# Neighbourhood attention: the scores are made two turns ahead, and queued on TensorE right in front of a turn's values

## The reference, cut to what matters

```python
z = h @ w_in[l]                                    # (1024, 1024) @ (1024, 2560)
a, gate, q, k, v = jnp.split(z, splits, axis=-1)
conv_out = conformer_conv(a, gate, ...)            # 31 taps over the positions, 512 channels
q = rms_norm(q.reshape(B, S, N_HEADS, HEAD_DIM), q_norm_g[l])
k = rms_norm(k.reshape(B, S, N_HEADS, HEAD_DIM), k_norm_g[l])
...
# each query sees an 8 x 16 window of keys, clamped inside the grid
s = jnp.einsum("bqhd,brqchd->bhqrc", q_r, k_win) * scale
s = s + bias                                       # learned, by 2-D offset
p = jax.nn.softmax(s, axis=(-2, -1))
out = jnp.einsum("bhqrc,brqchd->bqhd", p, v_win)
...
mix = jnp.concatenate([conv_out, attn_out], axis=-1)
x = x + mix @ w_out[l]
```

## Time and profile before

| what | value |
|---|---|
| median of 3 runs | 2429.26 us |
| the profiled execution | 2429.0 us, its span 2427.2 us |
| VectorE's first `scores_in` to its ninth (turn 0 to turn 8) | 146.15 to 216.43 us |
| pair 1, likewise | 216.43 to 287.52 us |
| pair 2, likewise | 287.52 to 359.77 us |
| from there to the first matmul that waits for the mixed input's low part | 359.77 to 442.26 us |

### The profile page before, as it was taken

One profiled execution on the slowest core, in us unless ns is written; L12 is line 12 of the kernel. 1 busy time (PEld: TensorE's weight loads), 2 busy tenths in 40 slices (PEclk: granted clock), 3 DMA queues, 4 the chain that ended last, 5 costly groups with the idle time before them and its releaser, 6 DMA issues. The chain is left out here.

```text
span 2427.2 us, 28938 instructions
## 1 busy us (share of the span) xinstructions
PE 2298.8 (95%) x10276; PEld 1765.5 (73%) x10276; DVE 1605.5 (66%) x1904; ACT 1096.1 (45%) x1779; POOL 1170.5 (48%) x834
## 2 busy tenths in 40 slices
PE   8988886899999999999999999997999999999999
PEld 6865553777888888788775665583788888888887
DVE  7888884288666666646766666747866665544587
ACT  5145554345545443322326666615666662222342
POOL 1000000257887787878521111232777777777732
PEclk9989997999999999999999999998999999999999
DMA  3211100421443436894310000032466668976412
GB/s 130 69 34 26 29 23 9 148 78 46 180 174 113 182 130 245 318 381 157 126 35 18 27 18 14 27 139 87 173 253 258 253 257 324 360 279 266 149 33 85
DMA packets 89166, 342.90 MB, mean 141 GB/s; under 512 B 22401, under 2 KB 23169, under 8 KB 76097
## 3 DMA queue, kind: packets, MB, share of 16 engines
q1 hardware_dynamic: 88368, 336.65, 36.8%
q10 hardware_dynamic: 656, 4.41, 0.5%
HBM read 224.16 MB, written 116.27 MB: 140 GB/s over the span
## 5 line engine op out<-in xcount | busy, mean ns | idle before, releaser
L1101 PE MATMUL ps<-operand,turn_weights 128*128 128x512 f32 x3192 | 736.3, 392 | 16.3 <-POOL turn_weights L728 5.5
L1101 PEld LDWEIGHTS ps<-operand,turn_weights 128*128 128x128 f32 x3192 | 600.6, 189 | 150.7 <-issue 14.4
L728 POOL TENSOR_TENSOR turn_weights<-turn_raw,turn_weights 128x512 fp32r<-128x512 f32 (+1 forms) x330 | 445.0, 1359 | 225.5 <-ACT turn_weights L1563 224.9
L1101 PE MATMUL ps<-hidden_operand,turn_weights 128*128 128x512 f32 x2268 | 517.5, 390 | 3.3 <-issue 1.4
L1101 PEld LDWEIGHTS ps<-hidden_operand,turn_weights 128*128 128x128 f32 x2268 | 424.8, 188 | 95.8 <-issue 6.0
L2756 DVE TENSOR_TENSOR branch_out<-ps,branch_out 128x1024 f32<-128x1024 f32 x172 | 210.5, 1224 | 201.3 <-PE ps L1101 200.3
L690 POOL TENSOR_TENSOR weight_hi<-weight_raw,zero_col 128x1024 fp32r<-128x1024 f32 (+1 forms) x27 | 54.6, 2023 | 582.1 <-PE ps L1007 409.8
L1563 ACT ACTIVATE turn_weights<-turn_raw 128x512 fp32r<-128x512 f32 (+1 forms) x330 | 204.9, 623 | 267.1 <-PE ps L1101 252.3
L842 PE MATMUL ps<-input_hi,weight_hi 128*128 128x512 f32 x592 | 196.2, 413 | 21.3 <-DVE input_lo L2335 10.4
L842 PE MATMUL ps<-input_lo,weight_hi 128*128 128x512 f32 x656 | 205.9, 395 | 0.0
L842 PE MATMUL ps<-input_hi,weight_lo 128*128 128x512 f32 x592 | 185.3, 395 | 0.0
(11 more groups left out here) (351 smaller groups left out, 3579.9 us busy)
## 6 DMA issues: line engine op xcount, KB each, us to landing
hidden_operand<-hidden_kept SPq DMA_DIRECT2D x91, 1024.0 KB, 7.8
hidden_kept<-hidden_parts SPq DMA_DIRECT2D x54, 1024.0 KB, 8.7
hidden_kept<-hidden_parts SPq DMA_DIRECT2D x27, 1536.0 KB, 6.2
turn_raw<-w_ff SPq DMA_DIRECT2D x40, 512.0 KB, 4.1
turn_raw<-w_mlp SPq DMA_DIRECT2D x32, 512.0 KB, 4.3
turn_raw<-w_mlpd SPq DMA_DIRECT2D x32, 512.0 KB, 4.4
turn_raw<-w_ffd SPq DMA_DIRECT2D x20, 512.0 KB, 4.6
weight_raw<-w_out SPq DMA_DIRECT2D x16, 512.0 KB, 3.6
```

Of the source, the lines that this page charges most:

```text
L728: pool_.tensor_tensor(place(p, 1), place(p, 1, WT) if raw is None else raw, bits(place(p, 0)), ALU.subtract).then_inc(s["st_lo"], 1)
L1101: ins = mm(PS[:, b, :], weights(p, w, k), tokens(p, a, k), start=(FRESH[p] and k == 0 and step == 0), stop=(k == n - 1 and step == 2), ski ...
```

## The change

`scores(n+2)`, no longer `scores(n+1)`, is made in turn n, and it stands behind the slots 0, 1 and 2, right in front of `values(n)`. Turn 6 makes none (the next pair's q and k aren't there), and turn 7 makes two: `scores(n+1)` behind `turn(n, 0)`, and `scores(n+2)` in front of `values(n)`. VectorE's `probs(n+1)` and `first_part` now stand ahead of `scores_in(n+2)`, and `second_part` behind it. ScalarE makes `exps(n+2)` at the end of a turn, and the `weight_hi` of a turn behind `head_guess`. The pieces, the taps and the transposes of v are dealt out anew, in the same number. In pair 3 `ln_sums` for the mean stands in turn 1 and not in turn 0.

```diff
-BESIDE = (((0, 1), (2,), (), (3,)),
+BESIDE = (((0,), (1,), (2,), (3,)),
           ((4,), (5,), (6,), (7,)),
           ((), (8, 9), (10,), ("m0", 11)),
-          ((12,), (13,), (14,), (15, "m1")),
-          ((), (16, 17), (), ("m2",)),
-          ((18,), (19,), (), ("m3",)),
-          ((20,), (21,), (), (22,)),
-          ((), (23,), (), ()))
+          ((12,), (13, "m1"), (14,), (15,)),
+          ((), (), (16,), ("m2", 17)),
+          ((18,), (19, "m3"), (20,), ()),
+          ((21,), (22,), (23,), ()),
+          ((), (), (), ()))
...
-            for what in BESIDE[0][0] + BESIDE[0][1] + BESIDE[0][3]:
+            for what in (0, 1):
                 next_piece(0, what)
             scores(0)
+            for what in (2, 3):
+                next_piece(0, what)
+            scores(1)
+            v_turn(0, 0)
...
+                    ahead = n + 2 < 4 * CBLOCKS
                     turn(n, 0)
-                    if j < CBLOCKS - 1:
+                    if ahead and j == 7:
                         scores(n + 1)
-                    if j == 1:
-                        v_turn(c, 1)
                     slot(0)
                     turn(n, 1)
+                    if j == 0:
+                        v_turn(c, 1)
                     slot(1)
                     if c == 3 and j >= 3:
                         output_part(j)
-                    if j == CBLOCKS - 1 and c < 3:
-                        scores(n + 1)
-                    if j == 0:
-                        v_turn(c, 0)
                     slot(2)
-                    values(n)
-                    slot(3)
-                    if c == 3 and j == 0:
+                    if ahead and j != 6:
+                        scores(n + 2)
+                    if c == 3 and j == 1:
                         ...
                         ln_sums(lambda m: Y[:, m, :], "ln_mean")
+                    values(n)
+                    slot(3)
+                    if j == CBLOCKS - 1 and c < 3:
+                        v_turn(c + 1, 0)
```

ScalarE, the order of a turn:

```diff
                     probs_t(n, 0)
-                    if more:
-                        exps(n + 1, 0)
-                        exps(n + 1, 1)
...
+                    if more and not new_pair:
+                        probs_scale(n + 1, 0)
                     probs_t(n, 1)
+                    if more and not new_pair:
+                        probs_scale(n + 1, 1)
...
                         if j == 2:
                             head_square(c + 1, 0)
-                            weight_hi(U_QKV + 3 * c + 5)
                         elif j == 4:
                             head_square(c + 1, 1)
-                            weight_hi(U_QKV + 3 * c + 6)
...
+                    if ahead and j < 6:
+                        exps(n + 2, 0)
+                        exps(n + 2, 1)
+                    elif new_pair:
+                        exps(n + 1, 0)
+                        exps(n + 1, 1)
                         probs_scale(n + 1, 0)
                         probs_scale(n + 1, 1)
+                        exps(n + 2, 0)
+                        exps(n + 2, 1)
                     if c < 3:
                         if j in (2, 3, 4, 5):
                             head_guess(4 * c + 2 + j, 5)
                         elif j == 6:
                             head_hi(c + 1, 1)
+                        if j == 2:
+                            weight_hi(U_QKV + 3 * c + 5)
+                        elif j == 4:
+                            weight_hi(U_QKV + 3 * c + 6)
                         elif j == 7:
                             weight_hi(U_QKV + 3 * c + 7)
```

More of the change, by code:

```diff
@@ L1062, in _ @@
                         ln_sums(lambda m: Y[:, m, :], "ln_mean")
-                    elif c == 3 and j == 3:
+                    values(n)
+                    slot(3)
+                    if j == CBLOCKS - 1 and c < 3:
+                        v_turn(c + 1, 0)
+                    if c == 3 and j == 3:
                         pe.wait_ge(s["ln_sq"], 4)
@@ L1702, in _ @@
             probs_scale(0, 1)
+            exps(1, 0)
+            exps(1, 1)
             for c in range(4):
@@ L1705, in _ @@
                     n = CBLOCKS * c + j
-                    more = n < 4 * CBLOCKS - 1
+                    more, ahead = n + 1 < 4 * CBLOCKS, n + 2 < 4 * CBLOCKS
+                    new_pair = more and j == 7
                     probs_t(n, 0)
-                    if more:
-                        exps(n + 1, 0)
-                        exps(n + 1, 1)
[L1711 to L1714, removed]
+                    if j == 0:
+                        v_copy(c, 0)
+                        if c:
+                            attn_out(c - 1, 0)
+                            attn_out(c - 1, 1)
+                    if more and not new_pair:
+                        probs_scale(n + 1, 0)
+                    probs_t(n, 1)
+                    if more and not new_pair:
+                        probs_scale(n + 1, 1)
+                    if j == 0:
                         v_copy(c, 1)
@@ L1739, in _ @@
                             head_hi(c + 1, 1)
+                        if j == 2:
+                            weight_hi(U_QKV + 3 * c + 5)
+                        elif j == 4:
+                            weight_hi(U_QKV + 3 * c + 6)
                         elif j == 7:
                             weight_hi(U_QKV + 3 * c + 7)
-                    elif j == 3:
+                    elif j == 2:
+                        for m in range(4):
+                            act.wait_ge(s["ln_cent"], m + 1)
+                            act_.activation(LT[m][:], Y[:, m, :], ACT.Square).then_inc(s["ln_sq"], 1)
+                    elif j == 4:
                         for h in range(2):
@@ L2369, in conv @@
             def conv(n):
-                for _ in range(n):
+                for _ in range(min(n, 4 * TAPS - tap[0])):
                     c, t = divmod(tap[0], TAPS)
@@ L2473, in _ @@
             probs(0, 1)
+            scores_in(1, 0)
+            scores_in(1, 1)
             conv(2)
             def first_part(c, j):
-                if j == 0 and c:
-                    weight_lo(U_QKV + 3 * c + 4)
+                if j == 0:
+                    if c:
+                        weight_lo(U_QKV + 3 * c + 4)
+                    conv(1)
                 elif j == 1:
-                    conv(1)
+                    conv(2)
                 elif j == 2:
                     evac(c + 1, 0, 0)
+                    conv(1)
                 elif j == 3:
@@ L2487, in first_part @@
                     evac(c + 1, 1, 0)
+                    head_norm(4 * c + 5, 5)
                 elif j == 5:
-                    weight_lo(U_QKV + 3 * c + 6)
                     head_norm(4 * c + 6, 5)
@@ L2492, in first_part @@
                     head_norm(4 * c + 7, 5)
-                elif j == 7:
-                    head_lo(c + 1, 1)
+                    conv(1)
             def second_part(c, j):
@@ L2498, in second_part @@
                     weight_lo(U_QKV + 3 * c + 5)
-                elif j == 4:
-                    head_norm(4 * c + 5, 5)
+                elif j == 5:
+                    weight_lo(U_QKV + 3 * c + 6)
                 elif j == 6:
                     head_lo(c + 1, 0)
-                elif j == 7:
-                    evac(c + 1, 2, 0)
-                conv(min((4, 4, 3, 3, 2, 3, 3, 4)[j], 4 * TAPS - tap[0]))
+                    conv(1)
+                    head_lo(c + 1, 1)
+                conv((3, 3, 2, 4, 3, 3, 0, 1)[j])
             def last_pair(j):
                 if j == 0:
+                    conv(4 * TAPS - tap[0])
                     weight_lo(U_OUT + 1)
-                    conv(4 * TAPS - tap[0])
                 elif j == 1:
@@ L2532, in _ @@
                     n = CBLOCKS * c + j
-                    more = n < 4 * CBLOCKS - 1
-                    if more and j < CBLOCKS - 1:
+                    if j == CBLOCKS - 1 and c < 3:
+                        conv(2)
                         scores_in(n + 1, 0)
                         scores_in(n + 1, 1)
+                        evac(c + 1, 2, 0)
+                        conv(1)
+                        probs(n + 1, 0)
+                        probs(n + 1, 1)
+                        scores_in(n + 2, 0)
+                        scores_in(n + 2, 1)
+                        second_part(c, j)
+                        continue
+                    if n + 1 < 4 * CBLOCKS:
+                        probs(n + 1, 0)
+                        probs(n + 1, 1)
                     if c < 3:
                         first_part(c, j)
[L2539 to L2546, removed]
+                    if j < 6:
+                        scores_in(n + 2, 0)
+                        scores_in(n + 2, 1)
                     if c < 3:
```

5 lines of the change are left out of this document (2 added, 3 removed).

## The result

The changed kernel takes 2475.09 us (median of 4 runs, 2469.78 to 2476.60) against 2429.43 (4 runs, 2428.68 to 2430.15): a ratio of 1.0185, with a 95% interval of 1.0173 to 1.0197. It is slower by 45.7 us. The prediction was 2467, with 2449 to 2485 as its range.

A forecast was written before the change was run, and what follows sets the result against it. VectorE and its waits were taken to set pairs 0 to 2. Start 6.0, pairs 10.1 and 9.0, pair 3 - 1.5 make + 23.6; with 15 for the clock, 2429.0 becomes 2467 us, range 2449 to 2485.

The forecast's parts named there:

- The step that carried it: Pairs 0 to 2: scores queue behind TensorE work that waits for VectorE; a pair takes 81.2 us against 71.09 and 72.25.
- turn 7 to 0: End of a pair: TensorE is behind, about 12.4 us against VectorE's own 8.2, so VectorE idles about 4.
- `weight_lo` was to idle 3.9 us: Turn 2 to 3: VectorE waits for weight_hi, now behind exps and head_guess; 3.9 us idle, before 1.94.
- Rival A: Pairs 0 to 2: TensorE gets ahead and VectorE never waits for scores; 2402 us, chance 0.06.
- Rival E: Whole kernel: no difference, pair 3 giving back the loss or waits already elsewhere; chance 0.05.
- The clock: Three TensorE gaps a pair, each followed by half speed on VectorE's path; 5.1 us a pair, 15 in three pairs.
- Rival B: Pairs 0 to 2: waits as worked out but the clock stays up; 2453 us, chance 0.25.
- D: Pairs 0 to 2: TensorE stays at half speed through most of each pair; 2484 us, chance 0.14.
- Pair 3: Last pair: layer norm's serial blocks stay and only change places; 81.0 us against 82.49, so 1.5 less.
- the start: Pair 0 up to turn 7: scores_in of turn 7 at 222.4 where before it was 216.43, + 6.0 us at full clock.
- Behind the stage: TensorE's and GpSimd's work after the mixed input: moved as a whole, no change in its length.
- turn 1 to 2: Scores stand behind pieces 8, 9 and 10, which wait for VectorE's evac; 11.6 us, VectorE idle 4.1.

The follow-up runs named there:

- e1: Changed kernel with scores(n+2) moved right behind turn(n, 1) and the transposes of v, ahead of slots 1 and 2; 2428.92 us, ratio 0.9992.
- e4: Changed kernel with 150 unused matmuls added in TensorE's gaps ahead of piece 8, "m1" and piece 16; 2456.28 us, ratio 1.0107.
- e2: Changed kernel with weight_hi of turns 2 and 4 right behind head_square again, ahead of exps and head_guess; 2452.11 us, ratio 1.0095.
- e3: Changed kernel with the scores moved behind turn(n, 1) and weight_hi of turns 2 and 4 back behind head_square; 2411.84 us, ratio 0.9929.
- e8: e7 with VectorE's norm of the convolution in pair 3 moved from turn 5 to turn 6; 2412.30 us, ratio 0.9931.
- e5: Kernel before the change, with weight_hi of turns 2 and 4 moved ahead of head_square; 2428.99 us, ratio 0.9997.
- e6: Changed kernel with only turn 2's scores moved ahead of slot 1, other turns' left in front of the values; 2468.49 us, ratio 1.0161.
- e7: e3 with turn 2's mean m0 moved behind piece 9 and weight_hi moved ahead of head_square; 2412.25 us, ratio 0.9922.

## Why the prediction was right

**The mechanism.** The step that carried it, scores queued behind matmuls that wait for VectorE itself, is shown by e1: with only that undone, the whole loss is gone. The table under e4 has its terms one by one, and the largest difference is 0.9 us, in turn 7 to 0. `weight_lo` was to idle 3.9 us and idles 3.75, and e2 shows that this wait was on the path. Rival A (the kernel gets faster, since TensorE gets ahead) failed where it was said to: the semaphore on piece 8. A gain of 17 us is there in e3, once nothing that waits for VectorE stands in front of the scores, but it isn't shown to come from the lead. Rival E (no difference) is out by the time itself.

**The clock.** It was taken as 5.1 us a pair and measured as 5.1, by the difference of e4 and the changed kernel in pair 1. Against that pair of e4, pair 2 of the changed kernel is 5.4 us longer and pair 0, from turn 0 to turn 7, 6.3: some 17 us in all, an estimate from these three differences, where 15 were taken. Rival B (the clock stays up) is out, as the windows at 0.74, 0.64 and 0.50 show, and D (half speed through most of a pair), as 0.86 does. There was luck in the term. I took it since gaps over 3 us were followed by half speed, and had the gaps at 3.3, 4.6 and 4.6 us. They came at 2.63, 3.77 and 2.88, so two of the three lie under the 3 us of my reason, and the clock fell behind them all the same.

**Pair 3.** It was to be 1.5 us shorter and is 2.4 shorter. The steps on the way came as listed, 1.2 to 1.4 us early: `scores_in(28)` after 26.2 us (27.6 worked out), the last `scores_in` done after 58.8 (60.0).

**Mis-sized: the start.** The `scores_in` that begins pair 1 was to come some 11 us later, 6.0 by the queues and 5 by the clock; it comes 15.7 later. The sum had the `scores_in` made in turn 0 at 153.6, and it starts at 156.58, 3.0 us later. Of these, 1.6 are there at the first `scores_in` already (147.76, before 146.15). They are no effect of the change: it starts at 145.6 to 146.0 in e1, e4 and e8, which have the changed kernel's order up to that point, and at 147.8 in e5, which has that of the kernel before. For the rest, I had put pieces 2 and 3 at no cost beside the scores; with them behind `scores(0)`, TensorE has a gap of 3.8 us ahead of `scores(0)`, and both pieces run partly at half speed after it.

```profile
145.68 0.39 PE L951 MATMUL ps<-k_hi,q_hi 64*128 64x256 f32 x2 [3.81 <-issue]
...
146.42 1.22 PE L842 MATMUL ps<-input_hi,weight_hi 128*128 128x512 f32 x2
```

The other 1.7 us lie between there and the start of pair 1. 1.2 of them are in turn 1 to 2, which takes 14.4 us in pair 0 and 13.2 in pair 1: the clock behind piece 8 stayed low for longer (0.63 from piece 8 to the `scores_in`, against 0.75 in pair 1).

**Behind the stage.** Nothing was to change there; it takes 0.9 us less, which is within what that part varies by from one execution to another (see e8).

**What was left out.** The prediction was made for one execution. The four runs of the changed kernel spread over 6.8 us, and the profiled one is the lowest; the 13 runs of the kernel before beside e1 to e4 spread over 7.4. Against the profiled 2469.8 the forecast is 3 us low, against the median of 2475 it is 8 low, about as far as rival D's 2484 is high. The three slower runs have a granted clock of 0.967 over the whole program and the profiled one 0.969, which points to more time at half speed; they have no trace that would show where.

## What to carry to other kernels

In queues written by hand, count for each result what stands ahead of it that waits for its own consumer. Here a second turn of lead didn't help: if one matmul in front of the scores waits for VectorE and VectorE waits for the scores, the lead is spent. A wait is worth what the next limit leaves of it: by the list of waits e6 should have given 17 us and gave 7 by the medians, e5 and e7 gave nothing, and e2 gave more than its wait because a gap of another engine closed with it.

## What the runs showed of the hardware

Gaps of 2.63 and 2.88 us on TensorE were followed by half speed in pair 1, shorter ones than the 3.1 of the earlier trace rows on which I had built. With e4's fillers, gaps of 1.2 to 1.8 us remained at the same places of pair 1, and the clock held. The length of the gap alone doesn't settle it. The first window below is e2's pair 2, behind a gap of 2.63 us ahead of piece 8; the second is e4's pair 2 at piece 16, where the fillers had a gap of 1.66 us ahead of them and left 0.92 behind them.

```profile
331.40:336.60 5.20, 5.20 (x28) 3.95 (x30) 1.05 (x2) 2.10 (x3) 0.00 (x0) 1.00 0.01 3
```
```profile
360.40:364.61 4.21, 4.21 (x14) 2.74 (x16) 1.92 (x4) 1.15 (x2) 0.00 (x0) 0.50 0.00 0
```

Another such stretch lies outside the attention. From VectorE's first split of the mixed input to its first residual sum, the windows of the kernel before, e3 and e7 are these.

```profile
440.89:453.44 12.55, 11.35 (x50) 9.30 (x50) 5.77 (x5) 3.75 (x4) 0.00 (x0) 1.00 0.46 179
```
```profile
420.50:434.45 13.95, 12.57 (x49) 10.36 (x50) 5.77 (x5) 3.76 (x4) 0.00 (x0) 0.88 0.51 197
```
```profile
423.25:438.65 15.40, 14.03 (x49) 11.36 (x50) 5.77 (x5) 3.75 (x4) 0.00 (x0) 0.78 0.57 222
```

The same work takes 12.55, 13.95 and 15.40 us, and TensorE's gap at its start was 1.21, 3.58 and 3.74 us. The long gap belongs to the changed order and not to a quicker attention: it is 3.44 us in the changed kernel itself, the slowest of all, and 3.3 to 4.7 in the seven experiments built on it, but 1.22 in e5, which has the order of the kernel before. In e3 and e7 the stretch gave back 1.4 and 2.9 us of what the attention had won.
